# Attention with three banks of probabilities: every third unit split on another engine, the stores in another queue, the products one unit further behind

## What is computed

```python
s = jnp.einsum('bqhd,bkhd->bhqk', q, k).astype(jnp.float32) * scale
decay = jnp.transpose(cq, (0, 2, 1))[:, :, :, None] - jnp.transpose(ck, (0, 2, 1))[:, :, None, :]
mask = pos_k[None, :] <= pos_q[:, None]
s = jnp.where(mask[None, None], s + decay, NEG_INF)
p = jax.nn.softmax(s, axis=-1)
return jnp.einsum('bhqk,bkhd->bqhd', p.astype(v.dtype), v)
```

## Time and profile before

| | |
|---|---|
| median of 3 runs | 2924.09 us (2922.81 to 2926.6) |
| the profiled execution: time, span | 2925.41 us, 2923.8 us |
| TensorE busy in the span | 2766.0 us, 95% |
| VectorE, ScalarE, GpSimd busy | 1271.9, 895.1, 927.0 us |
| attention stage | about 641 to 1166 us of the span |
| TensorE's mean granted clock | 0.978 |

### The profile page before, as it was taken

The page is one execution under the profiler, slowest core; times in us unless marked ns, Lnnn a source line. Parts: engine busy times, 40 slices in busy tenths (PEclk is TensorE's granted clock), DMA queues, the critical chain, the costliest instruction groups (busy, mean ns, idle before and its releaser), DMA issues.

```text
span 2923.8 us, 40223 instructions
## 1 busy us (share of the span) xinstructions
PE 2766.0 (95%) x14550; PEld 2424.5 (83%) x14550; DVE 1271.9 (44%) x2362; ACT 895.1 (31%) x1621; POOL 927.0 (32%) x613
## 2 busy tenths in 40 slices
PE   7999999999898988799699999999999999999997
PEld 6899899987777777588599999999987888888886
DVE  4333343348786777577423223232235223222235
ACT  3201201127676766455211111212122121121122
POOL 3233334211111111444233333333245333333333
PEclk9999999999999999899899999999999999999999
DMA  6543535674433333566910111111146111111113
GB/s 180 183 125 116 159 104 157 197 186 120 104 94 93 94 93 94 164 210 208 259 57 30 57 43 43 43 43 43 43 130 197 59 44 48 53 43 56 44 43 115
DMA packets 261442, 305.23 MB, mean 104 GB/s; under 512 B 19324, under 2 KB 221704, under 8 KB 256712
## 3 DMA queue, kind: packets, MB, share of 16 engines
q1 hardware_dynamic: 209272, 256.14, 29.6%
q0 software_dynamic: 14304, 21.63, 2.9%
q10 hardware_dynamic: 37744, 25.96, 2.8%
HBM read 221.21 MB, written 82.21 MB: 104 GB/s over the span
## 4 chain that ended last, share of the span: by engine, by line
PE 46%; DMA 2%; POOL 2%; DVE 1%; ACT 0%; issue 0%; SPq 0%; POOLq 0%
PE up_bank L2340 23%; PE dn_bank L2363 23%; DMA m_x_in<-scratch_x 1%; DVE y L2294 1%; POOL y L2158 1%; DMA m_h_lo<-scratch_h_lo 0%; POOL dn_lo L2138 0%; POOL up_lo L2138 0%; DMA m_x_in<-y 0%; DMA m_raw<-in_w_down 0%; POOL u_hl L2150 0%; DVE y L2281 0%; POOL m_h_hi L2130 0%; DVE up_lo L2297 0%; ACT dn_hi L2209 0%; ACT up_hi L2209 0%
## 5 line engine op out<-in xcount | busy, mean ns | idle before, releaser
L2363 PE MATMUL dn_bank<-dn_hi,u_hl 128*128 128x512 f32 x2112 | 671.5, 390 | 6.9 <-DVE y L2279 4.4
L2150 POOL TENSOR_TENSOR u_hl<-u,u_hl 128x64 fp32r<-128x64 f32 (+2 forms) x192 | 200.2, 1066 | 900.7 <-DVE u L2266 900.7
L2363 PEld LDWEIGHTS dn_bank<-dn_hi,u_hl 128*128 128x128 f32 x2112 | 397.1, 188 | 90.7 <-DVE y L2279 4.8
L2340 PE MATMUL up_bank<-m_h_hi,up_hi 128*128 128x512 f32 (+2 forms) x1280 | 452.6, 354 | 17.1 <-DVE up_lo L2297 11.3
L2340 PE MATMUL up_bank<-m_h_lo,up_hi 128*128 128x512 f32 (+2 forms) x1280 | 451.9, 353 | 0.0
L2340 PE MATMUL up_bank<-m_h_hi,up_lo 128*128 128x512 f32 (+2 forms) x1280 | 451.9, 353 | 0.0
L2219 ACT ACTIVATE u<-up_bank 128x512 f32<-128x512 f32 (+2 forms) x160 | 83.7, 524 | 1159.8 <-PE up_bank L2340 1153.5
L2281 DVE TENSOR_TENSOR y<-dn_bank,y 128x1024 f32<-128x1024 f32 x255 | 312.0, 1224 | 289.2 <-PE dn_bank L2363 289.1
L2363 PE MATMUL dn_bank<-dn_lo,u_hl 128*128 128x512 f32 x1088 | 424.6, 390 | 0.0
L2266 DVE TENSOR_TENSOR u<-u 128x512 f32<-128x512 f32 (+2 forms) x160 | 93.9, 628 | 698.0 <-ACT u_hl L2222 698.0
L504 POOL TENSOR_TENSOR w_lo<-w_raw,w_hi 128x1024 fp32r<-128x1024 f32 x72 | 181.3, 2522 | 336.1 <-DVE w_hi L722 336.1
(11 more groups left out here) (256 smaller groups left out, 4828.0 us busy)
## 6 DMA issues: line engine op xcount, KB each, us to landing
w_raw<-in_w_in SPq DMA_DIRECT2D x72, 512.0 KB, 4.1
m_raw<-in_w_up SPq DMA_DIRECT2D x32, 1024.0 KB, 5.4
m_raw<-in_w_down SPq DMA_DIRECT2D x32, 1024.0 KB, 4.8
nck<-scratch_ncum SPq DMA_DIRECT2D x9, 1312.0 KB, 18.6
scratch_v_hl<-vhl SPq DMA_DIRECT2D x20, 512.0 KB, 2.6
q_hi<-scratch_q_hi SPq DMA_DIRECT2D x18, 528.0 KB, 7.6
q_lo<-scratch_q_lo SPq DMA_DIRECT2D x18, 528.0 KB, 9.4
v_hl<-scratch_v_hl SPq DMA_DIRECT2D x9, 1024.0 KB, 20.7
```

The lines of the kernel that those rows point to most:

```text
L2150: rest = pool.tensor_tensor(u_hl[:, o % 2, b, to], u[:, b, at], u_hl[:, o % 2, b, at].bitcast(F32), ALU.subtract)
L2340: mm = pe.matmul(up_bank[2 * (o % 2) + b][:, 0:w], wp[:, c, k, b * P:(b + 1) * P], hp[g][s][:, k, :], start=(k == 0 and p == 0), stop=(k = ...
L2363: mm = pe.matmul(bank[:, cols], u_hl[:, o % 2, b, part], wp[:, c, b, cols], start=(b == 0 and p == 0), stop=(b == 1 and p == len(passes) - 1))
```

## The change

Five things change in `attend`; the other stages stay.

1. In groups 1 to 3 every third unit (n % 3 == 2, but for the last two of a group) is a side unit. ScalarE copies its `t_bank` as fp32 to `side_f`, which frees the bank. GpSimd makes `side_hi` by adding a zero column, and then `side_lo` by subtraction. There are 2 + 3 + 4 side units in a head, 72 in all, 64 of 512 columns and 8 of 384. VectorE does nothing for them.
2. `V_BEHIND` is 3. A side unit's V stands 6 units behind its T.
3. The N of a group goes in at place 2 of the next group's steps.
4. `att` has five buffers, and SyncE issues the stores, each when `att_done` says that GpSimd has multiplied. GpSimd waits for a buffer only.
5. GpSimd takes the list's steps with ScalarE's delays.

```diff
-V_BEHIND = 2
+V_BEHIND = 3
+P_BUFS = 3
+USED0 = P_BUFS + 1
+S_BUFS = 2
+SIDE_EVERY, SIDE_LATER = 3, 3
+A_BUFS = 5
...
+            turns.append(Step("T", par, off, g=g, blocks=blocks, cols=cols))
+            turns[n].side = 0 < g < extra and n % SIDE_EVERY == 2 and n < len(units) - 2
+        due = [n + V_BEHIND + (SIDE_LATER if t.side else 0) for n, t in enumerate(turns)]
...
-                    steps.insert(4, late)
+                    steps.insert(2, late)
...
             def step(it, x):
+                if x.kind == "N":
...
+                    sp.wait_ge(att_done, upto("N", it, x.at) + 1)
+                    sp.dma_start(dst.rearrange("(a p) (i c) -> p a i c", a=n, c=2 * HD)[:, :, it, x.off * HD:(x.off + 1) * HD],
+                                 att[rows, x.at % A_BUFS, 0:n, :]).then_inc(att_stored[x.at % A_BUFS], 16)
                 if x.kind != "L":
                     return
                 h = sp.snap((2 * it + x.off) % HEADS)
-                sp.wait_ge(used, T_BANKS + upto("V", it, v_read[x.off]))
+                sp.wait_ge(used, USED0 + upto("V", it, v_read[x.off]))
...
+            def split(it, x):
+                pool.wait_ge(side_out, side_upto(it, x.i) + 1)
+                pool.wait_ge(used, read_before(it, x, aside, S_BUFS))
+                width = x.cols.stop - x.cols.start
+                pool.tensor_tensor(side_hi[:, x.p, x.cols], side_f[:, x.p, x.cols], zero[:, :].to_broadcast([P, width]), ALU.add).then_inc(side_hi_done, 1)
+                pool.wait_ge(side_hi_done, side_upto(it, x.i) + 1)
+                pool.tensor_tensor(side_lo[:, x.p, x.cols], side_f[:, x.p, x.cols], side_hi[:, x.p, x.cols].bitcast(F32),
+                                   ALU.subtract).then_inc(side_lo_done, 1)
...
-                pool.dma_start(dst.rearrange("(a p) (i c) -> p a i c", a=n, c=2 * HD)[:, :, it, x.off * HD:(x.off + 1) * HD],
-                               att[rows, 0:n, :]).then_inc(att_stored, 16)
-                pool.wait_ge(att_stored, 16 * (upto("N", it, x.at) + 1))
-
-            loop(pool, "pool", step)
+
+            loop(pool, "act", step)
...
-                    act.wait_ge(used, upto("V", it, x.at) + 1)
-                    act.activation(p_hi[:, x.at % T_BANKS, x.cols], t_bank[x.at % T_BANKS][:, x.cols], ACT.Copy).then_inc(hi_done, 1)
+                    if x.side:
+                        act.wait_ge(side_lo_done, side_upto(it, x.i) + 1)
+                        act.activation(side_f[:, x.p, x.cols], t_bank[x.at % T_BANKS][:, x.cols], ACT.Copy).then_inc(side_out, 1)
+                    else:
+                        act.wait_ge(used, read_before(it, x, main, P_BUFS))
+                        act.activation(p_hi[:, x.p, x.cols], t_bank[x.at % T_BANKS][:, x.cols], ACT.Copy).then_inc(hi_done, 1)
...
-                    pe.wait_ge(lo_done, upto("T", it, x.at) + 1)
+                    before_it = turns[x.at - T_BANKS]
+                    if before_it.side:
+                        pe.wait_ge(side_out, side_upto(it, before_it.i) + 1)
+                    else:
+                        pe.wait_ge(lo_done, T_BANKS + main_upto(it, before_it.i + 1 - (len(main) if x.at < T_BANKS else 0)))
```

More of the change, by code:

```diff
@@ L1080, in __init__ @@
         self.v, self.o = v, o
-        self.at, self.free, self.exps, self.last_piece = None, None, None, None
+        self.side, self.i, self.read = False, None, None
+        self.at, self.free, self.exps, self.last_piece, self.p = None, None, None, None, None
 def attention_order():
@@ L1113, in products @@
             units = [((j,), max(0, j - 4 * g) * P) for j in range(4 * g + 4)]
+        turns = []
         for n, (blocks, col) in enumerate(units):
             cols = slice(col, 512) if g < extra else slice(0, len(blocks) * P)
-            t = Step("T", par, off, g=g, blocks=blocks, cols=cols)
-            steps.append(t)
-            behind.append(Step("V", par, off, g=g, t=t, first=n == 0, last=n == len(units) - 1))
-            if len(behind) > V_BEHIND:
-                steps.append(behind.pop(0))
-        return steps + behind + [Step("O", par, off, g=g, v=behind[-1])]
+            turns.append(Step("T", par, off, g=g, blocks=blocks, cols=cols))
+            turns[n].side = 0 < g < extra and n % SIDE_EVERY == 2 and n < len(units) - 2
+        due = [n + V_BEHIND + (SIDE_LATER if t.side else 0) for n, t in enumerate(turns)]
+        by_due = sorted(range(len(turns)), key=lambda n: (due[n], n))
+        steps, v = [], []
+        for n, t in enumerate(turns):
+            steps.append(t)
+            if len(v) < len(turns) and due[by_due[len(v)]] <= n:
+                v.append(Step("V", par, off, g=g, t=turns[by_due[len(v)]], first=not v))
+                steps.append(v[-1])
+        while len(v) < len(turns):
+            v.append(Step("V", par, off, g=g, t=turns[by_due[len(v)]], first=not v))
+            steps.append(v[-1])
+        v[-1].last = True
+        return steps + [Step("O", par, off, g=g, v=v[-1])]
     def mix(a, b):
@@ L1226, in attend @@
         att_done = sem("att_done")
-        att_stored = sem("att_stored")
+        att_stored = [sem(f"att_stored{i}") for i in range(A_BUFS)]
         before, body, start, per = attention_order()
+        turns = sorted((x for x in body if x.kind == "T"), key=lambda x: x.at)
+        main, aside = [x for x in turns if not x.side], [x for x in turns if x.side]
+        for x in body:
+            if x.kind == "V":
+                x.t.read = x.at
+        for group, n_bufs in ((main, P_BUFS), (aside, S_BUFS)):
+            assert len(group) % n_bufs == 0
+            for i, x in enumerate(group):
+                x.i, x.p = i, i % n_bufs
+        assert not any(x.side for x in turns[-T_BANKS:])
         QM = per["M"]
@@ L1251, in loop, with main_upto, side_upto, read_before @@
                     step(it, x)
+        def main_upto(it, n):
+            return len(main) * it + n
+        def side_upto(it, n):
+            return len(aside) * it + n
+        def read_before(it, x, group, n_bufs):
+            if x.i >= n_bufs:
+                return USED0 + upto("V", it, group[x.i - n_bufs].read + 1)
+            return USED0 + upto("V", it, group[x.i - n_bufs].read + 1 - len(turns)) if not x.side else USED0 + upto("V", it, 0)
         m_of = {}
@@ L1288, in _ @@
                 pool.sem_clear(s)
+            def split(it, x):
[6 more added lines that the diff above has]
+                                   ALU.subtract).then_inc(side_lo_done, 1)
             def step(it, x):
+                if x.kind == "T" and x.side:
+                    split(it, x)
                 if x.kind != "N":
@@ L1412, in step @@
                     t, o = x.t, o_of[x.off, x.g]
-                    pe.wait_ge(lo_done, T_BANKS + upto("T", it, t.at) + 1)
+                    hi, lo = (side_hi, side_lo) if t.side else (p_hi, p_lo)
+                    if t.side:
+                        pe.wait_ge(side_lo_done, S_BUFS + side_upto(it, t.i) + 1)
+                    else:
+                        pe.wait_ge(lo_done, T_BANKS + main_upto(it, t.i) + 1)
                     if x.first:
@@ L1421, in step @@
                             out, at, vb = o_bank[o % O_BANKS][:, 0:P], slice(i * P, (i + 1) * P), QT if j == CB else QT + 1 + j
-                        pe.matmul(out, v_hl[par][:, vb, :], p_hi[:, t.at % T_BANKS, at], start=x.first and i == 0, stop=False)
-                        mm = pe.matmul(out, v_hl[par][:, vb, :], p_lo[:, t.at % T_BANKS, at], start=False, stop=x.last and i == len(t.blocks) - 1)
+                        pe.matmul(out, v_hl[par][:, vb, :], hi[:, t.p, at], start=x.first and i == 0, stop=False)
+                        mm = pe.matmul(out, v_hl[par][:, vb, :], lo[:, t.p, at], start=False, stop=x.last and i == len(t.blocks) - 1)
                     mm.then_inc(used, 1)
```

42 lines of the change are left out of this document (27 added, 15 removed).

## The result

The changed kernel takes **2878.5 us** (median of 4 runs, 2877.7 to 2882.1). The kernel before, run on the same chip, took 2924.5. The ratio is 0.9845, with a 95% interval of 0.9828 to 0.9862: 46 us faster. I had forecast 2896, with a range of 2880 to 2914.

A forecast was written before the change was run, and what follows sets the result against it. TensorE was taken to bound the kernel, busy 470.0 of attention's 525 us, with its waits to win. Terms -16 - 12 - 4 + 3 = -29 against the profiled 2925.4 gave 2896 us, range 2880 to 2914.

The forecast's parts named there:

- the products' term: In attention, products three transposes behind instead of two shorten TensorE's waits for `p_lo`: -12 us, bounds -5 and -21.
- the side units': In attention, GpSimd takes every third unit; some side products wait, +0.4 us in each head: +3 us, bounds 0 and +24.
- stores on SyncE: At the loop's back edges, loads behind the store shorten ScalarE's pause and half the half-clock stretch: -16 us, bounds 0 and -30.
- N two places earlier: N's transposes fill the sample unit's wait, -3 us, and a late step fills group 0's start, -1 us.
- Rival 1: At the back edges, the fetch stays long, the 6.8 us pause being ScalarE's own: -13, 2912 us; chance 0.15.
- rival 2: In attention, more comes free: edges' half clock goes entirely, hidden waits count nearly in full: -43, 2882 us; chance 0.17.
- the edges: The attention loop's back edges, three between four iterations, were said to cost about 10 us each.
- hidden waits cost only in part: In attention, waits behind running matmuls count only partly, so the products were put at -12 us, near the lower bound.
- and needs none of them: In attention, VectorE loses about 49 us of work to the side units, and this was given no value.
- Rival 3: In attention's group 3, GpSimd becomes the new bound and side products wait, slower than before: 2931 to 2950 us; chance 0.09.
- a ScalarE pause above 6 us: At the back edges, a sign: the prediction is wrong if the pause is still over 6 us; near 2.9 was expected.

The follow-up runs named there:

- e9: The changed kernel with 120 filler instructions on TensorE ahead of the attention loop, 90 of them at TensorE's very start: 2872.1 us.
- e10: The kernel before with products three transposes behind and four buffers for them, nothing else changed: 2907.2 us.
- e3: The kernel before with attention's outputs stored from SyncE with five buffers, nothing else changed: 2905.6 us.
- e8: The changed kernel without side units, with four buffers and N back at its old place: 2883.8 us.
- e7: The changed kernel without side units, with four buffers and filler instructions on TensorE, 64 ahead of the loop and 192 behind: 2910.0 us.
- e6: The kernel before with filler instructions on TensorE, 64 ahead of the loop and 192 behind: 2965.0 us.
- e5: The changed kernel with filler instructions on TensorE, 120 ahead of the loop and 136 behind: 2890.3 us.

## Why the prediction was right in direction and wrong in size

All four terms of the sum came out more favourable than I had them, and one cost was not in it at all. The largest misses are the products' term (-12, measured -20.6), the side units' (+3, measured -7.6 once their code is not fetched again) and TensorE's own code fetch (nothing, measured +15.2). Each step adds one part to the row above, in attention, by the profiles:

| part | predicted, bounds | measured | how |
|---|---|---|---|
| stores on SyncE | -16, 0 to -30 | -20.3 | 523.0 to 502.7 |
| products further behind | -12, -5 to -21 | -20.6 | to 482.1 |
| N two places earlier | -4, 0 to -4.5 | -10.4 | to 471.7 |
| side units, their code not fetched again | +3, 0 to +24 | -7.6 | to 464.1 (e9) |
| TensorE's code fetched at each edge | not in the sum | +15.2 | to 479.3 |
| sum | -29 | -43.7 | |

The products' row also holds what little GpSimd's new delays (change 5) are worth; e10, which has the further products alone, gained 21.5.

**Stores.** The mechanism came as forecast: with the store ahead of the loads ScalarE's code comes in 2.3 us at most, where it took 6.8 behind them (with the open point named at e3). Rival 1 is out. The wait that is left is 1.6 to 1.8 us and not 2.4, and the half clock behind the edge goes whole at two edges and by half at the third, not by half at all three. It is the value that rival 2 gave to the edges, -20.

**Products further behind.** Off by 8.6 us, and the step that failed is "hidden waits cost only in part". I took the waits' rows (40.7 shown, 21.0 of the weight loads) for the stock of what can be won and paid the small ones a part. The matmuls' row is less than the stock: of what TensorE lost before products, 71 to 81 us by the count, it shows 40.7. With three behind (e10) 41 of it went, and 26 came back before transposes. The rest of the term is the clock. Behind the sample unit's pause it stays whole when products are three behind, though the pause is the same 1.38 us (e8, e10); half-clock stretches cost 15.4 us before and 8.3 in e10. I had not priced it.

**N.** I counted two places, the sample unit's wait and group 0. The starts of groups 2 and 3 win 0.3 us each too, and group 0's start wins 0.9 in each second head, where I had one microsecond for all heads together. The sample unit's wait gave 0.3 a head, near the 0.44 of the sum.

**Side units.** The costs were as worked out: GpSimd's pair takes 1.02 and 1.26 us, 164.2 in all for the some 175 predicted, and no product waits for `side_lo`.

```profile
L1354 POOL TENSOR_TENSOR side_lo<-side_f,side_hi 128x512 fp32r<-128x512 f32 (+1 forms) x72 | 91.0, 1264 | 5.6
L1352 POOL TENSOR_TENSOR side_hi<-side_f,zero 128x512 fp32r<-128x512 f32 (+1 forms) x72 | 73.2, 1017 | 28.1 <-ACT side_f L1389 22.6 <-PE o_bank L1499 5.4
```

What failed is that the term gave VectorE's 49 us no value ("and needs none of them") and added +3 for side products that wait. With the side units TensorE loses another 7.3 us less before products. Whether this is VectorE's relief or the longer way of the side products, six units behind, no run parts. Rival 3, GpSimd as the bound, is out. With the fetch that they bring counted to them, the side units cost attention 7.6 us in the changed kernel (471.7 to 479.3).

**The missing term.** I weighed the code fetch of ScalarE at length and never asked what the change does to TensorE's. The side units' kinds of waits take its body from 1612 to 1653 instructions; register operations (ALU_OP) went from 110 to 191 in an iteration and semaphore instructions from 100 to 58, and I had counted only operations with a duration. That costs 15.2 us, three pauses of 3.4 to 4.8 us and the half clock behind them, and hides most of the gain at the edges in the changed kernel: by the pause alone one would have judged that the stores did nothing. I named as what would make the prediction wrong a ScalarE pause above 6 us; it came (6.09), with another cause.

Rival 2 (2882) was the nearest: it has the edges and the hidden waits nearly in full, and there its mechanism is borne out. That its total is near as well is in part luck. It lacks the fetch (+15.2), and it gave too little to N (by 6.4 us) and to the side units (by 7.6), and these nearly cancel. Without the fetch the gain in attention would have been 58.9 us (523.0 to 464.1), twice what I forecast.

## What to carry to other kernels

A row of waits is not the stock of what more distance can win: take the starts of a busy engine's instructions and compare the intervals with those at full rate, which here showed 71 to 81 us where the row had 40.7. For a loop, count the body's instructions on each engine before and after a change, register and semaphore instructions too, and look for instruction packets in the later iterations; a body that has lost its place comes back by moving where it starts. At a back edge, try the next iteration's loads behind something late enough for the code fetches to be through; here that took 20 us off the attention stage.

## What the runs showed of the hardware that was not expected

- A loop body of 1612 instructions on TensorE stays loaded or is fetched in each iteration by a shift of 64 instructions (attention 523.0 and 541.2 us); one of 1653 the other way round by a shift of 120 (479.3 and 463.8).
- The fetch pauses TensorE for 3 to 5 us at an edge when the loads begin at about the same time or behind it (e7: 2.95; changed: 3.4 to 4.8) and for 5.8 and 5.2 us where they are already under way (e6, which differs in more than the loads). ScalarE's pause was 6.76 us under the loads and 2.27 ahead of them.
- An instruction of TensorE that holds two waits on a semaphore already set took 108 ns (136 of them in 14.7 us, e5).
- The same pause of 1.38 us is followed by half clock in the kernel before (0.67 over the 4.6 us behind it) and by a whole clock in e8 (1.00) and e10 (1.00 over 7 us). e10 differs from the kernel before only in the products' distance; what in the order of the work ahead of the pause does it was not tried.
